# Second attention: the reciprocal row sums go through memory instead of through TensorE

## The chip, the cores and the metric

The program runs on one core of a Trainium2 chip. The metric is the device time of one execution in microseconds; the median of three executions stands for the kernel. Five engines run their own instruction streams and meet through semaphores: TensorE (PE), VectorE (DVE), ScalarE (ACT), GpSimd (POOL) and SyncE (SP), which here only issues DMAs. "L133" in a row of the profile is line 133 of the kernel. The lines named most often are those of one-line helpers (L133 matmul, L136 transpose, L139 activation, L142 tensor_tensor, L157 tensor_copy, L163 reciprocal, L193 dma_start), so a row says which kind of instruction it is, and its place in time says which one.

## The reference

Two transformer blocks follow each other on a 1024 x 1024 input. The change lies in the attention of the second block: 16 heads of 64 values, a window of 384 keys around each block of 128 queries, 256 context keys, and one sink term per head in the softmax.

```python
def block(i):
    ...
    s_lat = jnp.einsum('bqhgd,bshd->bhgqs', qb, kb).astype(jnp.float32) * scale
    s_ctx = jnp.einsum('bqhgd,bshd->bhgqs', qb, k_ctx).astype(jnp.float32) * scale
    ...
    logits = jnp.concatenate([s_lat, s_ctx, sink_column(sink, s_lat.shape[:-1])], axis=-1)
    p = jax.nn.softmax(logits, axis=-1)
    ...
    return (jnp.einsum('bhgqs,bshd->bqhgd', p_lat, vb)
            + jnp.einsum('bhgqs,bshd->bqhgd', p_ctx, v_ctx))
```

The kernel leaves the division by the softmax's row sums to the end: it multiplies the values with exp(score - max) and scales the result by the reciprocal of each row sum.

## The kernel before

All order is written out by hand: each engine has a function for each stage, and a table of named events gives the semaphores. The second attention is the stage `mix_*`. It takes 64 steps `s`, each for one query block and two heads; eight steps make one query block `i`, and four steps make a group `g = s // 4` (16 groups, eight heads each). Steps run in pairs.

- **PE** (`mix_pe`): for each pair of steps, `qk2` makes the scores of the next pair into PSUM banks 0 to 4; `turn2` transposes 128 x 128 pieces of exp(score), four per call, into banks 5 and 7 in turn (`turn_bank`); `turn_fifth` does the fifth piece where a block has five key tiles (blocks 1 to 6). Between them `fill_part` puts matmuls of another product (the projection of the convolution branch, 128 x 512 by three per part) that accumulates in bank 6. Where `s % 4 == 0`, `values2` multiplies the turned pieces of the group before with the values, into bank 7. The results stand with heads and value dimensions on the partitions and the 128 queries along the row.
- **Row sums.** DVE's `row_sums2(g)` leaves the eight reciprocals of a group in `rinv`, with queries on partitions. The result of `values2` has queries along its rows, so the reciprocals must be turned. Before the change POOL copies them out into `rspread`, 128 x 512, each value 64 times (`o2_spread`), and PE's `sums2(g - 1)` turns this with four transposes, at the end of the first pair of steps of group g. DVE's `o2_normed(g - 1)` multiplies `on` (the result, taken from PSUM by ACT's `o2_take`) with the turned reciprocals in PSUM, at the start of the second pair of group g.
- **DVE** (`mix_dve`) runs in order: `o2_normed`, `sink_arg`, then `max2` (mask and row maximum of the next scores, out of banks 0 to 4) interleaved with the copies of turned pieces (`p2_evacuate`), then `row_sums2` and `pc_take` at the end of the second pair. PE's next `qk2` waits for the last `max2` of the pair before, since it takes its banks.
- **SP** (`mix_sp`) issues the loads of a gate tile (`gs_load`, 256 KB, waits for `pc_take` of two groups before) and of the next weights (`w_load`, 512 KB) in one queue. **POOL** (`mix_pool`) issues `pc_store`, 256 KB per group.

After this stage come the output projection (`proj_*`), the router and the 16 experts.

Of the kernel before, what the change touches and what calls it, by code (L numbers as in the profile page):

```python
# [7 lines left out]
F32 = mybir.dt.float32  # L8
F32R = mybir.dt.float32r
U32 = mybir.dt.uint32  # L10
ALU = mybir.AluOpType
# [38 lines left out]
    
# [4 lines left out]
    "x_row_sums": "x1_half x2_half", "rope_step": "rope_swap rope_cos rope_sin",  # L55
}
# [169 lines left out]
def program(  # L226
# [7 lines left out]
    with ctx:  # L234
# [3 lines left out]
        def new_sem(name):  # L238
# [3 lines left out]
            nc.dram_tensor(f"{n}_scratch", [1024, 1024], F32, kind="Internal").ap()  # L242
            for n in ("x1", "x2", "xh", "xa", "y", "sa", "sc"))
        pc_dram = nc.dram_tensor("pc_scratch", [1024, 1024], F32, kind="Internal").ap()
        q_dram = nc.dram_tensor("q_scratch", [1280, 1024], F32, kind="Internal").ap()
        c_dram = nc.dram_tensor("c_scratch", [8, 1024], F32, kind="Internal").ap()
        h_dram = nc.dram_tensor("h_scratch", [2816, 1024], F32, kind="Internal").ap()
# [23 lines left out]
        def sm(*dims):  # L271
            n = int(np.prod(dims))
            v = small[:, taken[0]:taken[0] + n]
            taken[0] += n
            assert taken[0] <= 584, taken
            return shaped(v, dims)
# [4 lines left out]
        def rr(kb, *dims):  # L281
            return shaped(piece(AR0 + kb, int(np.prod(dims)), F32R), dims)
# [66 lines left out]
        W_PC = len(WT)  # L349
# [15 lines left out]
        def w_raw(n):  # L365
            _, nk, cols_, _ = WT[n]
            return piece(8 * (n % 2), 2048, F32)[:, 0:nk * cols_].rearrange("p (k n) -> p k n", n=cols_)
# [8 lines left out]
        def w_load(sp, n):  # L376
            parts, nk, cols_, _ = WT[n]
            if n >= 2:
                sp.wait_ge("w_low", n - 2)
            for place, src in parts:  # L380
                sp.dma_start(place(w_raw(n)), src).then_inc(*sp.landed(f"w_raw{n % 2}", n))
# [68 lines left out]
        def ps(sem, *key):  # L450
            return PS[:, bank_of.get((sem, *key), 0), :]
# [315 lines left out]
        rinv = sm(16)  # L767
# [856 lines left out]
        hs = [tuple(rr(32 + 4 * j + a, 512) for a in (0, 2)) for j in range(4)]  # L1624
# [779 lines left out]
        LAST = NST - 1  # L2404
# [560 lines left out]
        amask, amask0, rspread = ar(48, 640), ar(50.5, 512), ar(52.5, 4, 128)  # L2965
# [26 lines left out]
        def yh_of(h, k):  # L2992
            return yh[8 * h + k]
# [16 lines left out]
        def y_low(e, h, k):  # L3010
            e.wait_ge("y_high", h, k)
            e.tensor_tensor(yl_of[h][:, k, :], yl_raw[h][:, k, :], yh_of(h, k).bitcast(F32), ALU.subtract).then_inc(
                *e.did(y_low_of(h), h, k))
# [26 lines left out]
        def gs_load(sp, n):  # L3040
            if n >= 16:
                return
            if n >= 2:
                sp.wait_ge("pc_out", n - 2)
            else:
                sp.wait_ge("st_acc", LAST, "P2")
                for x in range(4):
                    sp.wait_ge(f"g_st{x}", 7)
            sp.dma_start(gs[n % 2], sc_dram[tile128(n // 2), half512(n % 2)]).then_inc(*sp.landed(f"gl{n % 2}", "c", n))

        def mix_sp(sp):
            gs_load(sp, 0)
            gs_load(sp, 1)
            for j in range(8):
                gs_load(sp, 2 * j + 2)
                if j < 7:
                    w_load(sp, W_PC + j + 2)
                gs_load(sp, 2 * j + 3)

        QK_PIECES = ((0, 1, 384, 640), (1, 0, 256, 640), (0, 0, 0, 256), (1, 1, 256, 640), (0, 0, 256, 512), (0, 0, 512, 640),  # L3060
                     (1, 0, 0, 256), (0, 1, 0, 256), (1, 1, 0, 128), (0, 1, 256, 384), (1, 1, 128, 256))
# [60 lines left out]
        def sums2(pe, g):  # L3122

            b = turn_bank(pe)
            pe.take(b, "o2_out", g)
            bank_of["o2_sums", g] = b
            pe.wait_ge("o2_spread", g)
            for j in range(4):
                t = pe.transpose(PS[:, b, tile128(j)], rspread[:, j, :], ident)
            t.then_inc(*pe.did("o2_sums", g))  # L3130
# [15 lines left out]
        def mix_pe(pe):  # L3146
            pe.wait_ge("k_in")
            pe.wait_ge(*v2_out(4))
            pe.wait_ge(*v2_out(5))
            pe.wait_ge("kc_out_a")  # L3150
            pe.wait_ge("kc_out_v")
            qk2(pe, 0)
            for s in range(2):
                for k1 in range(2):
                    fill_part(pe, s, k1)
            for s in range(0, NS2, 2):
                if s + 2 < NS2:
                    qk2(pe, s + 2)
                if s and s % 4 == 0:
                    values2(pe, s // 4 - 1)  # L3160
                if s % 4 == 0:
                    pe.turn = 0
                for s_ in (s, s + 1):
                    for c in range(2):
                        turn2(pe, s_, c)
                        if s:
                            fill_part(pe, s_, c)
                if len(chunks2(s)) == 3:
                    turn_fifth(pe, s)
                pe.named("p2_turned", s)  # L3170
                pe.named("p2_turned", s + 1)
                if s and s % 4 == 0:
                    sums2(pe, s // 4 - 1)
            values2(pe, 15)
            pe.turn = 0
            sums2(pe, 15)
            pe.turn = 0
# [93 lines left out]
        def o2_normed(dve, g):  # L3271

            dve.wait_ge("o2_taken", g)
            dve.wait_ge("o2_sums", g)
            dve.tensor_tensor(q2_of(g // 2)[:, 4 * (g % 2):4 * (g % 2) + 4, :], on[g % 2].rearrange("p (k n) -> p k n", n=128),
                              ps("o2_sums", g).rearrange("p (k n) -> p k n", n=128), ALU.mult).then_inc(*dve.did("o2_out", g))

        def pc_take(dve, n):
            dve.wait_ge("pc_acc", n)
# [53 lines left out]
        def mix_pool(pool):  # L3333
            for s in range(NS2):
                for h, k in y_parts(s):
                    if h:
                        y_low(pool, h, k)
                if s % 4 == 3:
                    g = s // 4
                    hs = slice(8 * (g % 2), 8 * (g % 2) + 8)  # L3340
                    pool.wait_ge("o2_rinv", g)
                    if g:
                        pool.wait_ge("o2_sums", g - 1)
                    pool.tensor_copy(rspread.rearrange("p j (a d) -> p j a d", d=64),
                                     rinv[:, hs].rearrange("p (a j) -> p j a", j=4).unsqueeze(3).to_broadcast(
                                         [128, 4, 2, 64])).then_inc(*pool.did("o2_spread", g))
                    pc_store(pool, g)

        def pc_store(pool, n):
            pool.wait_ge("pc_out", n)  # L3350
            pool.dma_start(pc_dram[tile128(n // 2), half512(n % 2)], pcb[n % 2]).then_inc(*pool.landed(f"pc_st{n % 2}", n))
# [975 lines left out]
        rows, ssr, rsr = xg, sm(3), sm(1)  # L4327
# [239 lines left out]
```

## Time and profile before

| | |
|---|---|
| median of 3 runs | 2761.48 us (2761.33 to 2762.14) |
| the profiled execution | 2762.24 us, span 2760.5 us |
| PE busy over the span | 2712.5 us, 98% |
| DVE busy | 1988.2 us, 72% |
| ACT busy | 1304.8 us, 47% |
| POOL busy | 547.1 us, 20% |
| granted TensorE clock | 0.996 of full speed on the mean |
| the chain that ended last | PE 86%, DVE 6%, DMA 2%, ACT 2%, issue 2%, POOL 2% |

The execution's own time is 1.7 us above its span: what lies around the first and last instruction. The busy share of PE is an average over all stages; how much of it is on the path in the second attention, from about 1664 to 1968 us, is read from the rows further down.

### The profile page before, as it was taken

Reading aid. Unit: us, or ns where it says so; the run is one execution under the profiler, and the core shown is the slowest. Engines: PE = TensorE matmul, PEld = TensorE weight load, DVE = VectorE, ACT = ScalarE, POOL = GpSimd, SP = SyncE. Lnnn points to the kernel's source line nnn. Section 1 sums busy time; section 2 is a strip of 40 time slices with the busy share of each in tenths; the row PEclk is TensorE's granted clock in tenths of the full one; section 3 lists DMA queues with packets and bytes.
Section 4 is the critical chain, followed back from the end, with each engine's and each line's share of the span. In section 5 each row is a group of like instructions: output and inputs, shape, how many; then the busy total and the mean of one; then the engine's idle time right before and its main releaser. Section 6 shows DMA issues by size and latency. Waiting matters only on the chain.

```text
span 2760.5 us, 35397 instructions
## 1 busy us (share of the span) xinstructions
PE 2712.5 (98%) x13762; PEld 2182.8 (79%) x13762; DVE 1988.2 (72%) x2820; ACT 1304.8 (47%) x2040; POOL 547.1 (20%) x512
## 2 busy tenths in 40 slices
PE   8999999999999999999999999999999899999998
PEld 7777778777778888988888887777788678888886
DVE  5344455888776588978867656666666889999997
ACT  5444533433333454443222236555423477777775
POOL 0011011645545111520011112000100410000000
PEclk9999999999999999999999999999999999999999
DMA  5111113344662898324312244011574699999998
GB/s 172 35 47 31 46 57 135 107 137 143 186 183 70 313 313 236 118 88 111 107 62 77 80 149 139 31 47 39 172 264 152 233 402 396 397 396 396 396 396 299
DMA packets 270634, 494.12 MB, mean 179 GB/s; under 512 B 30140, under 2 KB 141908, under 8 KB 269956
## 3 DMA queue, kind: packets, MB, share of 16 engines
q1 hardware_dynamic: 240864, 396.40, 41.2%
q0 software_dynamic: 29456, 95.43, 10.6%
q8 instruction: 109, 1.79, 0.3%
q14 instruction: 57, 0.47, 0.1%
q10 hardware_dynamic: 148, 0.04, 0.0%
HBM read 424.60 MB, written 67.21 MB: 178 GB/s over the span
## 4 chain that ended last, share of the span: by engine, by line
PE 86%; DVE 6%; DMA 2%; ACT 2%; issue 2%; POOL 2%; POOLq 0%; SPq 0%; DVEq 0%; ACTq 0%
PE PS L133 80%; PE PS L136 6%; DVE m L142 4%; ACT m L139 2%; POOL m L142 2%; DVE m L148 1%; DMA m<-h_scratch 1%; DMA m<-xh_scratch,small 0%; DMA m<-in_w_mod_dram 0%; DMA xa_scratch<-m,small 0%; ACT L139 0%; DVE m L151 0%; DVE m L145 0%; DMA m<-in_w_exp_up_dram 0%; DMA m<-in_x_dram 0%
## 5 line engine op out<-in xcount | busy, mean ns | idle before, releaser
L133 PE MATMUL PS<-m,m 128*128 128x512 f32 (+6 forms) x11722 | 2507.8, 387 | 10.2 <-DVE m L142 5.0
L133 PEld LDWEIGHTS PS<-m,m 128*128 128x128 f32 (+2 forms) x11722 | 1961.8, 183 | 465.1 <-issue 76.5
L139 ACT ACTIVATE m<-m 128x512 fp32r<-128x512 f32 (+4 forms) x887 | 797.2, 919 | 880.5 <-DVE m L142 379.3
L142 DVE TENSOR_TENSOR m<-m,m 128x512 fp32r<-128x512 f32 (+5 forms) x912 | 986.3, 1112 | 211.5 <-ACT m L139 189.9
L139 ACT ACTIVATE m<-PS 128x512 f32<-128x512 f32 (+4 forms) x495 | 278.2, 588 | 388.1 <-PE PS L133 188.1
L142 DVE TENSOR_TENSOR m<-PS,m 128x512 f32<-128x512 f32 (+1 forms) x454 | 299.8, 684 | 177.6 <-PE PS L133 119.8
L142 POOL TENSOR_TENSOR m<-m,m 128x512 f32<-128x512 f32 (+4 forms) x178 | 278.5, 1569 | 603.3 <-DVE m L142 273.3
L136 PE MATMUL PS<-ident,m 128*128 128x128 f32 x1722 | 245.1, 277 | 22.8 <-DVE m L145 8.6
L136 PEld LDWEIGHTS PS<-ident,m 128*128 128x128 f32 x1722 | 199.7, 141 | 76.6 <-issue 28.5
L139 ACT ACTIVATE m<-m,small 128x640 f32<-128x640 f32 (+5 forms) x203 | 157.6, 780 | 117.3 <-DVE small L151 116.5
L157 DVE COPY m<-PS 128x512 f32<-128x512 f32 (+2 forms) x148 | 95.4, 648 | 142.0 <-PE PS L136 116.3
L148 DVE SCALAR_TENSOR_TENSOR m<-m,small,m 128x512 f32<-128x512 f32 (+1 forms) x154 | 168.2, 1116 | 4.3 <-DMA x_scratch<-m 1.7
L151 DVE CUSTOM_DVE_ANT_0 m<-PS,m,small 128x640 f32<-128x640 f32 (+1 forms) x128 | 102.3, 845 | 26.7 <-PE PS L133 26.7
L148 DVE SCALAR_TENSOR_TENSOR m<-m,vecT,m 128x512 fp32r<-128x512 f32 (+3 forms) x96 | 63.4, 715 | 53.4 <-ACT m L139 52.8
L142 POOL TENSOR_TENSOR m<-m 128x512 f32<-128x512 f32 x62 | 83.9, 1361 | 30.0 <-DMA m<-in_w_gate_up_dram 17.8
L151 DVE CUSTOM_DVE_ANT_0 m<-PS,m 128x1024 f32<-128x1024 f32 (+7 forms) x64 | 45.9, 754 | 58.8 <-PE PS L133 58.8
L199 POOL DMA_INDIRECT m<-xh_scratch,small x17 | 22.2, 1308 | 253.3 <-PE PS L136 246.8
L142 DVE TENSOR_TENSOR m<-m,PS 128x512 f32<-128x512 f32 x75 | 50.8, 684 | 28.7 <-PE PS L133 15.9
L199 POOL DMA_INDIRECT xa_scratch<-m,small x15 | 27.4, 1827 | 208.6 <-DVE m L148 208.6
L139 ACT ACTIVATE m<-m,vecT 128x512 fp32r<-128x512 f32 (+2 forms) x80 | 41.3, 599 | 44.3 <-PE PS L133 44.2
L157 POOL COPY m<-small 128x512 f32<-128x512 f32 x16 | 9.9, 616 | 254.7 <-DVE small L163 254.7
L142 DVE TENSOR_TENSOR m<-m 128x512 f32<-128x512 f32 (+1 forms) x57 | 40.7, 714 | 0.1
(107 smaller groups left out, 547.3 us busy)
## 6 DMA issues: line engine op xcount, KB each, us to landing
m<-in_w_exp_gate_dram SPq DMA_DIRECT2D x64, 1024.0 KB, 15.2
m<-in_w_exp_up_dram SPq DMA_DIRECT2D x64, 1024.0 KB, 14.7
m<-in_w_exp_down_dram SPq DMA_DIRECT2D x64, 1024.0 KB, 15.0
m<-in_w_mod_dram SPq DMA_DIRECT2D x48, 512.0 KB, 3.8
m<-in_w_gate_up_dram SPq DMA_DIRECT2D x44, 512.0 KB, 6.6
m<-in_w_in_dram SPq DMA_DIRECT2D x21, 1024.0 KB, 5.2
m<-in_w_in_dram SPq DMA_DIRECT2D x25, 512.0 KB, 5.2
x_scratch<-m POOLq DMA_DIRECT2D x24, 512.0 KB, 3.8
```

The lines of the kernel that those rows point to most:

```text
L133: return Unsent() if self.e is None else self.e.matmul(o, l, r, start=first, stop=last, **k)
L136: return Unsent() if self.e is None else self.e.transpose(o, i, ident)
L139: return Unsent() if self.e is None else self.e.activation(o, i, fn, **k)
L142: return Unsent() if self.e is None else self.e.tensor_tensor(o, a, b, op)
L148: return Unsent() if self.e is None else self.e.scalar_tensor_tensor(out=o, in0=a, scalar=s, in1=b, op0=op0, op1=op1, **k)
L151: return Unsent() if self.e is None else self.e.tensor_tensor_reduce(**k)
L157: return Unsent() if self.e is None else self.e.tensor_copy(o, i)
L199: return Unsent() if self.e is None else self.e.indirect_dma_start(*a, **k)
```

## The change

For the groups 0 to 14, the spreading by POOL and the four transposes by PE go. SP gets three DMAs per group in their place: `spread_store` writes the 128 x 8 values of `rinv` as eight rows of 128 into a scratch tensor in memory, and `spread_load` reads rows 0 to 3 back onto partitions 0 to 63 and rows 4 to 7 onto partitions 64 to 127 of `rspread`, 2 KB per partition. `o2_normed` multiplies with `rspread` in SBUF instead of a PSUM bank. Group 15 keeps the old way. `pe.turn`, which picks bank 5 or 7, is set back at every pair of steps and no longer at every second.

```diff
+        rs_dram = nc.dram_tensor("rs_scratch", [8, 128], F32, kind="Internal").ap()
...
+        def spread_store(sp, g):
+            if g > 14:
+                return
+            sp.wait_ge("o2_rinv", g)
+            if g:
+                sp.wait_ge("rs_in", g - 1, 1)
+            with nc.allow_non_contiguous_dma(reason="eight values of each partition go to eight rows"):
+                sp.dma_start(rs_dram.rearrange("r q -> q r"), rinv[:, 8 * (g % 2):8 * (g % 2) + 8]).then_inc(
+                    *sp.landed("rs_st", g))
+
+        def spread_load(sp, g):
+            if g > 14:
+                return
+            sp.wait_ge("rs_st", g)
+            if g:
+                sp.wait_ge("o2_out", g - 1)
+            else:
+                sp.wait_ge("st_acc", LAST, "P2")
+            for a in range(2):
+                sp.dma_start(rspread[64 * a:64 * a + 64].rearrange("p j n -> p (j n)"),
+                             rs_dram[4 * a:4 * a + 4].rearrange("r q -> (r q)").partition_broadcast(64)).then_inc(
+                    *sp.landed("rs_in", g, a))
+
         def mix_sp(sp):
             gs_load(sp, 0)
             gs_load(sp, 1)
             for j in range(8):
-                gs_load(sp, 2 * j + 2)
-                if j < 7:
-                    w_load(sp, W_PC + j + 2)
-                gs_load(sp, 2 * j + 3)
+                for g in (2 * j, 2 * j + 1):
+                    spread_store(sp, g)
+                    gs_load(sp, g + 2)
+                    spread_load(sp, g)
+                    if g % 2 == 0 and j < 7:
+                        w_load(sp, W_PC + j + 2)
...
-                if s % 4 == 0:
-                    pe.turn = 0
+                pe.turn = 0
...
-                if s and s % 4 == 0:
-                    sums2(pe, s // 4 - 1)
...
             dve.wait_ge("o2_taken", g)
-            dve.wait_ge("o2_sums", g)
+            if g < 15:
+                dve.wait_ge("rs_in", g, 1)
+                inverses = rspread
+            else:
+                dve.wait_ge("o2_sums", g)
+                inverses = ps("o2_sums", g).rearrange("p (k n) -> p k n", n=128)
             dve.tensor_tensor(q2_of(g // 2)[:, 4 * (g % 2):4 * (g % 2) + 4, :], on[g % 2].rearrange("p (k n) -> p k n", n=128),
-                              ps("o2_sums", g).rearrange("p (k n) -> p k n", n=128), ALU.mult).then_inc(*dve.did("o2_out", g))
+                              inverses, ALU.mult).then_inc(*dve.did("o2_out", g))
...
+                if s == 63:
+                    pool.wait_ge("o2_rinv", 15)
+                    pool.wait_ge("o2_out", 14)
+                    pool.tensor_copy(rspread.rearrange("p j (a d) -> p j a d", d=64),
...
                 if s % 4 == 3:
-                    g = s // 4
-                    hs = slice(8 * (g % 2), 8 * (g % 2) + 8)
-                    pool.wait_ge("o2_rinv", g)
-                    if g:
-                        pool.wait_ge("o2_sums", g - 1)
-                    pool.tensor_copy(rspread.rearrange("p j (a d) -> p j a d", d=64),
...
-                    pc_store(pool, g)
+                    pc_store(pool, s // 4)
```

On PE, in a block with five key tiles, this is what stands between the first and the second pair of a group, with the semaphores waited for. `m_178` and `m_180` hold exp(score) of the fifth pieces, `m_176` is `rspread`, and `m_147` by `m_124` is the first matmul of `qk2`.

```order
@@ -6781,6 +6779,4 @@
 L136 MATMUL PS<-ident,m_178 128x128
 L136 MATMUL PS<-ident,m_180 128x128
-L136 MATMUL PS<-ident,m_176 128x128 [waits s_o2_spread,s_p_out_v]
-L136 MATMUL PS<-ident,m_176 128x128 x3
 L133 MATMUL PS<-m_147,m_124 128x256 [waits s_s_max]
```

Four transposes go and nothing takes their place; `qk2` follows `turn_fifth` directly, with the wait that it had.

On SP, this is the queue from the second gate tile to the first loads of group 1. `small` is where `rinv` lies, `m_208` and `m_209` are the gate tiles, and `s_y_dma` and `s_x_dma` count the new store and the new loads.

```order
 L193 DMA m_209<-sc_scratch 128x512
+L193 DMA rs_scratch<-small 128x8x1 [waits s_o2_rinv]
 L193 DMA m_208<-sc_scratch 128x512 [waits s_pc_out]
+L193 DMA m_176<-rs_scratch 64x512 [waits s_y_dma]
+L193 DMA m_176<-rs_scratch 64x512
 L193 DMA m_148<-in_w_proj_conv_dram 128x8x128 [waits s_w_low]
+L193 DMA rs_scratch<-small 128x8x1 [waits s_x_dma,s_o2_rinv]
 L193 DMA m_209<-sc_scratch 128x512 [waits s_pc_out]
+L193 DMA m_176<-rs_scratch 64x512 [waits s_o_out,s_y_dma]
+L193 DMA m_176<-rs_scratch 64x512
```

The store goes ahead of the gate tile's load; the two loads go behind it and ahead of the weights' load, and they wait for the store to land.

On DVE, the rows of `o2_normed` (the multiplication into `m_124`) between the copies of the first pair and `sink_arg` and `max2` of the second:

```order
 L157 COPY m_186<-PS 128x4x128 [waits s_o_acc,s_p_turned]
 L157 COPY m_186<-PS 128x4x128 [waits s_p_turned]
-L142 TENSOR_TENSOR m_124<-m_49,PS 128x512 [waits s_o2_sums,s_o2_taken]
+L142 TENSOR_TENSOR m_124<-m_49,m_176 128x512 [waits s_x_dma,s_o2_taken]
 L142 TENSOR_TENSOR small<-small 128x8 [waits s_s_max]
```

Its place is the same; it now waits for the loads' semaphore instead of PE's.

## Rows read from the trace of the kernel before

**Rows 1.** Windows: the 280 us of the stage's steady part
```profile
core 0: us, PE busy (x) PEld busy (x) DVE busy (x) ACT busy (x) POOL busy (x), PEclk, DMA share, GB/s
1680.00:1960.00 280.00, 280.00 (x1866) 204.39 (x1863) 171.75 (x378) 152.08 (x341) 22.88 (x35) 1.00 0.14 45
```
**Rows 2.** Chain of waits, one group: start us, us, what, instructions
```profile
1823.79 0.87 PE PS L136 x8
1824.66 2.37 PE PS L133 x18
...
1831.69 0.44 PE PS L136 x4
```
**Rows 3.** Groups by shape in 1680 to 1960: count, busy, mean ns
```profile
L142 DVE TENSOR_TENSOR m<-m,PS 128x512 f32<-128x512 f32 x15 | 10.3, 689 | 12.7 <-PE PS L136 12.7
```
**Rows 4.** Timeline of DVE, groups 7 and 8: start, duration, [idle before]
```profile
1813.16 0.20 DVE L163 RECIPROCAL small<-small 128x8 f32<-128x8 f32 x1
1813.28 0.68 DVE L142 TENSOR_TENSOR m<-PS,m 128x512 f32<-128x512 f32 x1
...
1823.14 0.69 DVE L157 COPY m<-PS 128x512 f32<-128x512 f32 x1 [1.56 <-PE PS L136]
1824.77 0.69 DVE L142 TENSOR_TENSOR m<-m,PS 128x512 f32<-128x512 f32 x1 [0.94 <-PE PS L136]
1825.38 0.16 DVE L142 TENSOR_TENSOR small<-small 128x8 f32<-128x8 f32 x1
1827.09 0.88 DVE L151 CUSTOM_DVE_ANT_0 m<-PS,m,small 128x640 f32<-128x640 f32 x1 [1.55 <-PE PS L133]
...
1830.19 0.88 DVE L151 CUSTOM_DVE_ANT_0 m<-PS,m,small 128x640 f32<-128x640 f32 x1
...
1832.96 0.20 DVE L163 RECIPROCAL small<-small 128x8 f32<-128x8 f32 x1
```
**Rows 5.** Timeline of POOL and of SP's queue, after the reciprocal
```profile
1813.43 0.62 POOL L157 COPY m<-small 128x512 f32<-128x512 f32 x1 [18.43 <-DVE small L163]
...
1813.99 20.12 SPq L193 DMA_DIRECT2D m<-sc_scratch  x2
```
**Rows 6.** Issue (ns) and landing of w_gate_up's loads, then of sc_scratch's
```profile
L193 SPq DMA_DIRECT2D m<-in_w_gate_up_dram x44: 367/548/882, 417.2 to 861.6; - x44
...
DMA to landing us min/median/max: 4.0/6.6/10.2
...
L193 SPq DMA_DIRECT2D m<-sc_scratch x16: 320/320/2758, 1671.2 to 1932.4; - x16
...
DMA to landing us min/median/max: 2.3/3.0/7.1
```
**Rows 7.** DMA queues over the whole span: packets, MB, share of 16 engines
```profile
q1 hardware_dynamic: 240864, 396.40, 41.2%
q0 software_dynamic: 29456, 95.43, 10.6%
```
**Rows 8.** Groups by shape on DVE in 1960 to 2050
```profile
L142 DVE TENSOR_TENSOR m<-m,m 128x512 f32<-128x512 f32 x14 | 9.7, 693 | 0.5
```
**Rows 9.** Timeline of DVE, groups 14 and 15
```profile
1948.92 0.20 DVE L163 RECIPROCAL small<-small 128x8 f32<-128x8 f32 x1
...
1960.99 0.69 DVE L157 COPY m<-PS 128x512 f32<-128x512 f32 x1 [0.73 <-PE PS L136]
```
**Rows 10.** Timelines of SP's queue and of ACT: two weights' loads, their first users
```profile
1794.55 0.43 SPq L193 DMA_DIRECT2D m<-in_w_proj_conv_dram  x1
...
1832.03 1.04 ACT L139 ACTIVATE m<-m 128x1024 fp32r<-128x1024 f32 x1
...
1932.74 21.07 SPq L193 DMA_DIRECT2D m<-in_w_proj_attn_dram  x8
...
1968.29 7.29 ACT L139 ACTIVATE m<-m 128x512 fp32r<-128x512 f32 x13
```
**Rows 11.** Issues of the experts' gate weights: first and last start
```profile
L193 SPq DMA_DIRECT2D m<-in_w_exp_gate_dram x64: 367/368/1057, 2113.9 to 2682.3; - x64
```

More of the change, by code:

```diff
@@ L3337, in mix_pool @@
                         y_low(pool, h, k)
-                if s % 4 == 3:
-                    g = s // 4
-                    hs = slice(8 * (g % 2), 8 * (g % 2) + 8)
-                    pool.wait_ge("o2_rinv", g)
-                    if g:
-                        pool.wait_ge("o2_sums", g - 1)
-                    pool.tensor_copy(rspread.rearrange("p j (a d) -> p j a d", d=64),
-                                     rinv[:, hs].rearrange("p (a j) -> p j a", j=4).unsqueeze(3).to_broadcast(
-                                         [128, 4, 2, 64])).then_inc(*pool.did("o2_spread", g))
-                    pc_store(pool, g)
+                if s == 63:
+                    pool.wait_ge("o2_rinv", 15)
+                    pool.wait_ge("o2_out", 14)
+                    pool.tensor_copy(rspread.rearrange("p j (a d) -> p j a d", d=64),
+                                     rinv[:, 8:16].rearrange("p (a j) -> p j a", j=4).unsqueeze(3).to_broadcast(
+                                         [128, 4, 2, 64])).then_inc(*pool.did("o2_spread", 15))
+                if s % 4 == 3:
+                    pc_store(pool, s // 4)
         def pc_store(pool, n):
```

2 rows, old and new, of the table SHARED are left out of this document.

## The prediction

> **What bounds the kernel now.** I read first how full each engine is in this stage, then the chain that ended last, then the engines' own timelines around one group.
>
> In the stage's steady part PE is busy for 280.00 of 280 us at full granted clock, DVE for 171.75, ACT for 152.08, and the DMA engines for 0.14 of their time [rows 1]. So PE is the only engine without idle time here, and the chain of waits agrees: inside a group it stays on PE from end to end. At the place of the change it shows eight transposes in one piece, the four of `turn_fifth` and the four of `sums2`, for 0.87 us, and `qk2` right behind; at the end of the next pair, where there is no `sums2`, four transposes take 0.44 us [rows 2]. What is taken off PE there is therefore on the path, as long as nothing that PE waits for comes later than now.
>
> What PE waits for next runs through DVE. The reciprocal of group 7 starts at 1813.16 and ends at 1813.36; `o2_normed(7)` starts at 1824.77, after 0.94 us of waiting for PE's transposes; `sink_arg` follows, and then DVE waits 1.55 us for the scores before `max2` starts at 1827.09 [rows 4]. That wait is the cushion behind `o2_normed`. The other cushion is ahead of it: from 1813.36 until DVE has finished the copy of 1823.14 (1823.83) there are 10.5 us in which nobody asks for the turned reciprocals.
>
> **What is removed.** On PE, four transposes for each of 15 groups. The chain gives 0.87 - 0.44 = 0.43 us for one group, and 0.44 for four transposes alone [rows 2]. 15 x 0.435 = 6.5 us, all on the path. On POOL, 15 spreads of 0.62 us [rows 5]; POOL is idle for 18.43 us ahead of each, so this is worth nothing.
>
> **What is exchanged on DVE.** `o2_normed` reads `rspread` from SBUF instead of a PSUM bank. With PSUM it takes 689 ns [rows 3]; the same shape with both operands in SBUF takes 693 ns in the next stage [rows 8]. 15 x 0.004 = 0.06 us on an engine that waits: nothing. The bank changes of `pe.turn` are nothing too: in blocks 1 to 6 the pairs before used 5, 7, 5, 7, 5 and then 7 for the sums, and the next pair began with 5 again, so dropping the 7 leaves the rest as it was. In blocks 0 and 7 the second pair now begins with 5 instead of 7, a bank whose last copy is three fills and a `qk2` old.
>
> **What is added: a longer way from `rinv` to `rspread`.** It has these steps.
>
> 1. SP wakes and issues the store. POOL's spread started 0.07 us after the reciprocal's end, SP's gate load 0.03 us after `pc_take`'s end (1813.28 + 0.68 = 1813.96, issue 1813.99) [rows 4, 5]. I take 0.1 us.
> 2. The store lands, L us after its issue. No DMA here writes pieces of 4 bytes. It has 128 x 8 = 1024 pieces, 64 for each of the 16 DMA engines. A load of `w_gate_up` also has 1024 pieces (512 KB in runs of 128 values) and lands in 4.0 us at least, 6.6 in the middle; the shortest landing of a 256 KB tile, with 128 pieces, is 2.3 us [rows 6]. Lower end: 2.3 us, since the data are next to nothing. Upper end: the 2.3 us and 64 pieces at the price of a mean packet. A packet of the hardware queue costs 0.412 x 16 x 2760.5 / 240864 = 0.0755 us, one of the software queue 0.106 x 16 x 2760.5 / 29456 = 0.159 us [rows 7], which makes 4.8 or 10.2 us of pieces, and L = 7.1 or 12.5 us. I take L = 4.0 us, the row with the same number of pieces with least beside it, as the DMA engines are nearly idle here [rows 1].
> 3. The gate tile's load stands between store and loads; its condition (`pc_take`) is met 0.6 us after the reciprocal, long before the store has landed. Nothing.
> 4. SP wakes (0.03), issues the first load (0.32), then the second, which lands after the 3.0 us that a gate tile takes in the middle [rows 6]: 3.35 us.
>
> The way is 0.1 + L + 3.35 = L + 3.45 us, so 7.5 us with L = 4.0. `rspread` is then ready at 1813.36 + 7.5 = 1820.8. DVE comes to `o2_normed` at 1823.83 less the 0.44 us by which PE is now ahead, 1823.4. It does not wait; even the 0.94 us that it waited for PE goes.
>
> **How much of L is free.** DVE does not wait at all up to L = 10.0 - 3.45 = 6.6 us. If it waits, what stands behind it is `sink_arg` and `max2`. The latest harmless start of `o2_normed` is 1827.09 - 0.44 - 0.61 - 0.16 = 1825.88, 12.5 us after the reciprocal. Behind it DVE runs without a gap until the last `max2` ends at 1830.19 + 0.88 = 1831.07, and PE's `qk2`, which needs it, starts at 1831.69 + 0.44 = 1832.13 [rows 2, 4]: 1.05 us more. So PE loses nothing up to 13.55 us, or L = 10.1. The groups of blocks 0 and 7 are shorter. For group 14 the reciprocal ends at 1949.12 and DVE's next copy after `o2_normed` and `sink_arg` (0.77 together) starts at 1960.99 [rows 9]: 11.1 us, 10.7 with PE ahead, so L = 7.2 before that copy is late, and about 1 us more before PE is. I expect the same of groups 0 and 13.
>
> **What is moved in SP's queue.** The weights' load now stands behind the loads of even groups, some L + 1 us later than before. The load issued at 1794.55 is first used by ACT at 1832.03, 37 us later [rows 10]. After group 14 the projection's second load can no longer be issued at 1932.74, it comes behind the loads of group 14: 1949.12 + 0.1 + 4.0 + 0.7, about 1954. Its first user on ACT stands in the run that starts at 1968.29 [rows 10]; 14 us cover a landing of 6.6. With L = 12.5 it would still be 5 us before. Nothing.
>
> **What comes after.** The first expert weights are asked for at 2113.9 [rows 11], after this stage, and everything later starts from its end, so the rest shifts as a whole.
>
> **Sum.** 2761.48 - 6.5 = 2755.0 us as a median. The profiled execution took 2762.24 us with a span of 2760.5, 0.8 above the median; one like it would show 2755.7 and a span of 2754.0.
>
> **A rule against the change.** What the rows say of the store is in step 2: no packet here costs more than 0.159 us on the mean of its queue [rows 7], and with that the loss is small or none. The Trainium skill says (VectorE: DVE Perf Modes, "The three transpose paths") that a plain DMA that transposes by its strides is 19 times slower than the transposing path, where the innermost destination stride is large, which is what the store does. With that page's 1.3 us for the fast path the store would take about 25 us, an estimate from the page alone; no run here shows it.
>
> **Rivals.**
>
> - *The store's narrow writes are slow, and DVE waits (ends slower).* Place: `o2_normed`, with `sink_arg` and `max2` behind it, and PE's `qk2` behind those. For it: no such DMA is in the trace, and DVE serves nobody while it waits. Against it: 64 pieces per DMA engine would have to cost over (10.1 - 2.3) / 64 = 0.12 us each. At 0.159 us, L = 12.5 is 2.4 us over in 12 groups and about 4.3 in the three short ones: 41.7 - 6.5 = 35 us slower, 2797. It breaks even at 6.5 / 15 = 0.43 us over per group, L = 10.5. Chance 0.10. *In an extreme form* a piece costs 0.35 us, twice the dearest mean: L = 2.3 + 22.7 = 25, 15 us over in 15 groups, 223 - 6.5: 2978 us. Chance 0.02. That is the size that the Trainium skill's rule of 19 times gives.
> - *The freed time is lost elsewhere (no change).* PE comes 0.44 us sooner to its next waits, and one of them fills it. For it: all engines hang on each other here. Against it: the only wait directly behind is that of `qk2` on a `max2` from the pair before, and DVE sat idle for 0.94 and 1.55 us in between [rows 4]. 2761.5 us, chance 0.05.
> - *Half of it.* The short groups are late by some tenths, or the later stages give back a part, as the DMA traffic of the experts falls otherwise: 2757 to 2760. Chance 0.10.
> - *More than counted*, from the shorter wait at `o2_normed` or POOL's quiet: below 2754. Chance 0.03.
>
> **How the numbers follow.** The forecast, 2755.0 with 2754 to 2756.5 as its own range, has 0.70. Two executions of this kernel agree within 0.03%, and I count 0.2%, 5.5 us, as the least that can be told from no change; the border is 2755.96, only 1 us above the forecast. So of the 0.70 I give 0.62 to faster by over 0.2% and 0.08 to within it; with 0.03 of the larger gain faster has 0.65. Within 0.2%: 0.08 + 0.10 + 0.05 = 0.23. Slower: 0.12. The range from 2753.5 to 2760.0 leaves out the slow store, no change and a little of the rest, 0.2 in all.
>
> **What would show it.** Right: between the pairs of a group PE has four transposes and `qk2` right behind, PE stays busy for all of the steady part, and the reciprocals of two groups in blocks 1 to 6 lie 19.36 us apart instead of 19.80 (1813.16 to 1832.96) [rows 4]. `o2_normed` has no wait for a DMA; the store lands in 3 to 6 us. Wrong in its size: the store lands in over 6.6 us and `o2_normed` shows a wait for the load, though PE doesn't. Wrong in sign: the store lands in over 10 us, PE waits for DVE at `qk2`, and the groups lie over 19.80 us apart.

## The result, and the profile after

The changed kernel takes 2816.47 us (median of 4 executions, 2815.3 to 2820.19) against 2761.68 before: 1.0198 times as long, interval 1.0186 to 1.0211, so 55 us slower where 6.5 us faster was forecast. Its profiled execution took 2820.19 us with a span of 2818.2.

The stage is where it went. The windows of the changed kernel, to compare with [rows 1]:

```profile
core 0: us, PE busy (x) PEld busy (x) DVE busy (x) ACT busy (x) POOL busy (x), PEclk, DMA share, GB/s
1680.00:1700.00 20.00, 16.07 (x93) 11.88 (x91) 8.59 (x21) 9.60 (x22) 5.92 (x7) 0.88 0.28 66
1700.00:1960.00 260.00, 231.08 (x1425) 166.09 (x1424) 132.16 (x293) 120.97 (x259) 6.28 (x12) 0.94 0.25 45
1960.00:2025.00 65.00, 56.30 (x328) 37.33 (x326) 30.12 (x71) 28.01 (x64) 2.23 (x4) 0.95 0.37 61
```

PE, full before, is idle for 41.5 of 345 us, its granted clock is below 1, and the DMA engines are busier (0.25 against 0.14) while they move as little. The experts' first load, which answers to [rows 11], starts at 2171.7 instead of 2113.9: all of the 57.7 us between the two spans is lost by then.

```profile
L193 SPq DMA_DIRECT2D m<-in_w_exp_gate_dram x64: 367/368/1453, 2171.7 to 2740.5; - x64
```

The list of waits from 1680 to 2020 says for whom (waiter, who was waited for, us in total, times, longest):

```profile
DVE m L142 <- DMA m<-rs_scratch: 86.8, 15, 6.9
...
PE PS L136 <- DVE m L157: 39.0, 14, 3.9
```

DVE waits 15 times for the loads of the reciprocals, 5.8 us each, and behind it PE waits 14 times for a copy on DVE, 2.8 us each. The chain of waits shows what the way from `rinv` is made of (start, us, what), for one group:

```profile
1815.89 10.33 DMA rs_scratch<-small
1826.22 0.02 issue
1826.24 0.45 SPq L193
1826.69 0.04 issue
1826.73 5.72 DMA m<-rs_scratch
...
1832.54 0.10 DVE m L142
```

The store takes 10.33 us, over all groups 9.9 to 12.3; then the second load takes 5.72. From the first load's issue to `o2_normed` it is 6.3 us here and in the middle of the groups, and 3.8 to 6.8 over all of them. From the reciprocal's end at 1815.86 to `o2_normed` at 1832.54 it is 16.7 us, 3.1 more than the 13.55 that were worked out as free. DVE's timeline has the wait where [rows 4] had 0.94 us for PE:

```profile
1825.64 0.69 DVE L157 COPY m<-PS 128x512 f32<-128x512 f32 x1 [1.56 <-PE PS L136]
1832.54 0.69 DVE L142 TENSOR_TENSOR m<-m,m 128x512 f32<-128x512 f32 x1 [6.21 <-DMA m<-rs_scratch]
1833.15 0.16 DVE L142 TENSOR_TENSOR small<-small 128x8 f32<-128x8 f32 x1
```

PE's timeline has the consequence, 2.95 us of waiting at a `turn2` that takes bank 7, with DVE's copy out of it still behind two `max2`:

```profile
1830.21 0.60 PE L136 MATMUL PS<-ident,m 128*128 128x128 f32 x4
...
1835.58 1.12 PE L136 MATMUL PS<-ident,m 128*128 128x128 f32 x4 [2.95 <-DVE m L157]
1836.35 1.63 PE L133 MATMUL PS<-m,m 128*128 128x512 f32 x3
1837.77 1.01 PE L136 MATMUL PS<-ident,m 128*128 128x128 f32 x4
1838.71 6.88 PE L133 MATMUL PS<-m,m 64*128 64x256 f32 x42
```

The four transposes after the wait take 1.12 us, those before it 0.60. A window over these shows the clock (columns as above):

```profile
1832.60:1835.50 2.90, 0.03 (x1) 0.00 (x0) 2.90 (x8) 1.56 (x4) 0.00 (x0) 0.95 0.09 25
1835.50:1838.70 3.20, 3.12 (x11) 2.46 (x11) 2.23 (x6) 2.59 (x7) 0.00 (x0) 0.51 0.00 0
```

PE stood still for 2.9 us and then worked at 0.51, the lower of its two levels (1.2 GHz), for 3.2 us; in the windows before (1829.0 to 1832.4) and after (1838.7 to 1845.0) it has 1.00, the full 2.4 GHz. From 1835.58 to 1838.71 it needs 3.13 us for what takes 1.66 in the kernel before (from the transposes at 1810.60 to `qk2` at 1812.26). So this group costs 2.95 for the wait and 1.5 for the clock. Not every group pays for the clock. Windows laid behind each of the 15 waits of the stage (40.0 us together) show the lower level behind 11 of them; behind the waits of 0.92, 1.99 and 0.99 us it stayed at the full one, and also behind one of the longest, 3.69 us (PE's timeline, and a window with the columns as above):

```profile
1741.55 0.65 PE L136 MATMUL PS<-ident,m 128*128 128x128 f32 x4 [3.69 <-DVE m L157]
```

```profile
1741.55:1748.55 7.00, 7.00 (x47) 4.55 (x49) 6.41 (x16) 4.26 (x11) 0.54 (x1) 1.00 0.07 1
```

Over the stage the three windows at the top give the bill: 41.5 us of idle PE, and 20 x 0.12 + 260 x 0.06 + 65 x 0.05 = 21 us for the clock, less the 6.5 us of the transposes: 56 of the 57.7 us. The stores of 12 groups lie between 1721.36 and 1981.61, 23.7 us apart, against 19.37 when nothing waits (below): 4.3 us more per group.

### The profile page after: what moved, and what is told of

Same layout as the page of the kernel before. It is cut to its first block, busy times and chain, and to the rows that moved or that the text cites. A ratio compares the mean times of both kernels' runs of the same rounds, so it can differ in the third digit from the quotient of the medians.

```text
span 2818.2 us, 35306 instructions
## 1 busy us (share of the span) xinstructions
PE 2728.4 (97%) x13702; PEld 2190.0 (78%) x13702; DVE 1985.9 (70%) x2820; ACT 1309.7 (46%) x2040; POOL 537.6 (19%) x497
## 3 DMA queue, kind: packets, MB, share of 16 engines
q0 software_dynamic: 29456, 95.43, 10.5%
## 4 chain that ended last, share of the span: by engine, by line
PE 75%; DMA 10%; DVE 9%; issue 3%; ACT 2%; POOL 1%; SPq 0%; POOLq 0%; DVEq 0%; ACTq 0%
PE PS L133 71%; DMA rs_scratch<-small 6%; DVE m L142 4%; PE PS L136 4%; DMA m<-rs_scratch 3%; ACT m L139 1%; DVE m L151 1%; DVE m L148 1%; POOL m L142 1%; DVE m L157 1%; DMA m<-in_w_down_dram 0%; DVE m L187 0%; DVE m L190 0%; DMA m<-xh_scratch,small 0%; DMA m<-in_w_mod_dram 0%
## 5 line engine op out<-in xcount | busy, mean ns | idle before, releaser
L142 DVE TENSOR_TENSOR m<-m,m 128x512 fp32r<-128x512 f32 (+4 forms) x927 | 996.5, 1105 | 296.6 <-ACT m L139 190.6
L136 PE MATMUL PS<-ident,m 128*128 128x128 f32 (+1 forms) x1662 | 246.1, 283 | 64.6 <-DVE m L157 41.5
L136 PEld LDWEIGHTS PS<-ident,m 128*128 128x128 f32 (+1 forms) x1662 | 197.0, 144 | 124.0 <-DVE m L157 49.1
L151 DVE CUSTOM_DVE_ANT_0 m<-PS,m,small 128x640 f32<-128x640 f32 (+1 forms) x128 | 102.3, 846 | 11.4 <-PE PS L133 11.2
L193 POOL DMA_DIRECT2D pc_scratch<-m x16 | 8.7, 544 | 307.4 <-DVE m L142 307.2
L142 DVE TENSOR_TENSOR m<-m,PS 128x512 f32<-128x512 f32 x60 | 40.5, 684 | 15.9 <-PE PS L133 15.9
```

The source lines that it names most:

```text
L136: return Unsent() if self.e is None else self.e.transpose(o, i, ident)
L142: return Unsent() if self.e is None else self.e.tensor_tensor(o, a, b, op)
L151: return Unsent() if self.e is None else self.e.tensor_tensor_reduce(**k)
L193: return Unsent() if self.e is None else self.e.dma_start(o, i)
```

## The experiments

Where a kernel leaves something out, its expectation says it. The kernel before ran beside each on the same chip (medians 2762.03 to 2762.31), and the ratios are against it. Of each store the table at the end gives the time from its issue to the first load's issue, both rows of SP's queue, for groups 1 to 14; it is called the store's time here.

**The store in pieces of 32 bytes** (e1_wide)

```diff
-                sp.dma_start(rs_dram.rearrange("r q -> q r"), rinv[:, 8 * (g % 2):8 * (g % 2) + 8]).then_inc(
...
+            sp.dma_start(rs_dram.rearrange("r (a b) -> (r a) b", b=8), rinv[:, 8 * (g % 2):8 * (g % 2) + 8]).then_inc(
...
```

> The changed kernel with one edit: the store writes each partition's eight reciprocals as one piece of 32 bytes (128 pieces), so the rows read back hold them in another order and the output is not the reference's. Same bytes, same waits, same loads. Theory A (the 1024 pieces of 4 bytes are what makes the store take 10 to 12 us): the store lands in 2 to 3 us, the loads after it in about 3.3, o2_normed does not wait, and the time is that of the first forecast, 2755 (2754 to 2757). Theory B (two DMAs behind each other through memory are too slow in any form, or share the queue with too much): the store stays above 6 us or the loads above 5, and the time stays above 2780. Gate tile loads, 13 us in the changed kernel, fall back to 3 us by A.

2755.81 us, ratio 0.9976 (0.9967 to 0.9986). The loads follow the store's issue by 1.4 us (less than the 2 to 3 expected), the gate tile's loads land in 3.0 us in the middle again, no wait for the reciprocals' loads is left, and PE is busy for 279.82 of the 280 us. The same two hops with the same bytes are hidden: theory A holds, B is out.

**No DMAs at all** (e2_no_dma)

```diff
-                    spread_store(sp, g)
                     gs_load(sp, g + 2)
-                    spread_load(sp, g)
...
-                dve.wait_ge("rs_in", g, 1)
                 inverses = rspread
```

> The changed kernel without the store and the loads: o2_normed of groups 0 to 14 multiplies with a tile that is set to 1.0 once, so the division by the row sums is left out for these groups. It measures the gain term alone. Theory A (PE's 60 transposes were all on the path at 0.435 us per four, and nothing else takes their place): 6.5 us faster than before, 2755.2 (2754.5 to 2756), groups of blocks 1 to 6 19.36 us apart. Theory B (the freed PE time is lost to another wait): 2760 or more, with a PE wait in the trace at qk2 or turn2.

2757.6 us, ratio 0.9983 (0.9974 to 0.9992), 4.5 us faster with an interval of 2.2 to 7.2 that holds the 6.5; the median lies above the range of theory A (2754.5 to 2756). The timeline measures the term more sharply. Two reciprocals in a row:

```profile
1810.27 0.20 DVE L163 RECIPROCAL small<-small 128x8 f32<-128x8 f32 x1
...
1829.64 0.20 DVE L163 RECIPROCAL small<-small 128x8 f32<-128x8 f32 x1
```

19.37 us instead of 19.80 [rows 4], 0.43 per group as read from [rows 2], and the span of the profiled execution is 2754.3 against 2760.5. The gain term was right.

**The kernel before, with the store added** (e3_before_store)

```diff
+                    spread_store(sp, g)
                     gs_load(sp, g + 2)
...
+            if g >= 2:
+                dve.wait_ge("rs_st", g - 2)
```

DVE's added wait keeps `rinv` from being overwritten before it is stored.

> The kernel before, with its four transposes kept, and the store of 1024 narrow pieces added for groups 0 to 14; nobody reads what it writes. Theory A1 (the loss comes only through DVE's wait for the loads): 2761.7, within 2 us of before, although the store lands in 10 us or more. Theory A2 (the narrow store also costs by holding up the DMA engines for the other transfers): the gate tile's load and pc_store land in 10 us or more as in the changed kernel, but since they are wanted two groups later, the time still stays within 3 us of before; over 2770 would say that the hold-up itself costs.

2761.78 us, ratio 0.9997 (0.9988 to 1.0007). The gate tile's loads land in 12.8 us in the middle between 1700 and 1960 us (3.0 before) and `pc_store` in 13.1 (3.5 before), but the gate tiles are wanted two groups later, and what `pc_store` writes only in the next stage. The narrow stores hold up the other transfers, and that alone costs nothing here: A1 holds, and of A2 the hold-up is there, without a cost.

**DVE turns, then four stores** (e4_dve_turn)

```diff
+            dve.reciprocal(rp[:, g % 2, 0:8], rinv[:, hs]).then_inc(*dve.did("dve_order~"))
+            dve.wait_ge("dve_order~")
+            dve.blocks_turned(rt[:, g % 2, :], rp[:, g % 2, :]).then_inc(*dve.did("o2_rinv", g))
...
+            for b in range(4):
+                sp.dma_start(rs_dram[:, 32 * b:32 * b + 32], rt[32 * b:32 * b + 8, g % 2, :]).then_inc(
+                    *sp.landed("rs_st", g, b))
```

> The changed kernel with the turning done by DVE ahead of the store: the eight reciprocals stand in 32 columns, DVE turns the four 32 x 32 blocks in one instruction, and four stores of 8 pieces of 128 bytes each write the rows; loads and everything else as in the changed kernel, and the whole computation is kept. Theory A: DVE pays about 0.2 us per group, the last of the four stores lands about 1.1 + 2.5 us after the first issue, rspread is ready some 8 us after the reciprocal, inside the 10 us that are free, and the time is 2755 (2754 to 2757.5), faster than both kernels. Theory B (any round trip through memory is too slow here): above 2770, with o2_normed waiting for the loads.

2755.8 us, ratio 0.9977 (0.9968 to 0.9986): faster than both kernels, with the whole computation. SP's queue and DVE:

```profile
1810.14 1.30 SPq L196 DMA_DIRECT2D rs_scratch<-m  x4
1811.48 0.34 SPq L196 DMA_DIRECT2D m<-sc_scratch  x1
1812.35 1.09 SPq L196 DMA_DIRECT2D m<-rs_scratch  x2
```

```profile
1809.90 0.21 DVE L181 STREAM_TRANSPOSE m<-m 128x32 f32<-128x32 f32 x1
...
1819.65 0.69 DVE L157 COPY m<-PS 128x512 f32<-128x512 f32 x1 [1.56 <-PE PS L136]
1820.26 0.68 DVE L142 TENSOR_TENSOR m<-m,m 128x512 f32<-128x512 f32 x1
```

The turn costs 0.21 us, the loads are issued 2.2 us after the first of the four stores, and `o2_normed` follows the copy without a wait.

**The pieces 512 bytes apart** (e5_apart)

```diff
+                sp.dma_start(rs_apart[:, :, 0], src).then_inc(*sp.landed("rs_st", g))
```

> The changed kernel with the store's 1024 pieces of 4 bytes written 512 bytes apart, each to a stretch of its own in a larger scratch tensor; the loads wait for it as before but read rows that only group 0 wrote, so the output is not the reference's. Theory C (the writes are slow because neighbouring pieces of one row, from different DMA engines, meet in the same stretch of memory): the store lands in 2.5 to 4 us and the time is about 2756. Theory D (each 4-byte write to memory costs about (10.3 - 2.3) / 64 = 0.125 us on its DMA engine wherever it goes): the store still takes about 10 us and the time stays near 2816.

2756.67 us, ratio 0.9978 (0.9968 to 0.9988). There are still 1024 pieces of 4 bytes, and one partition's eight stand 512 bytes apart in memory, as in the changed kernel, but the next partition's piece is 4096 bytes away and not 4; the loads follow the store's issue by 3.4 us. Theory D, the price per piece on its DMA engine, is out; it matters where the pieces go.

**Four of eight values** (e6_half)

```diff
+                sp.dma_start(rs_dram[0:n].rearrange("r q -> q r"), rinv[:, 8 * (g % 2):8 * (g % 2) + n]).then_inc(
...
```

> The changed kernel, but from group 1 on the store writes four of the eight values of each partition (512 pieces of 4 bytes), so the other four rows stay those of group 0 and the output is not the reference's. Theory D (price per piece): the store lands in 2.3 + 32 x 0.125 = 6.3 us, rspread is ready some 11 us after the reciprocal, DVE waits about 1 us and PE not at all, and the time is 2755 to 2758. Theory E (a fixed price for a store of such a form, whatever its number of pieces): 9 us or more, and the time stays above 2800.

2782.12 us, ratio 1.0066 (1.005 to 1.0081). Half the pieces take nearly as long, 10.0 us in the middle: D is out here too. Theory E has the store right and the time wrong (over 2800 expected). The time is shorter than the changed kernel's mostly through the loads: from the first load's issue to `o2_normed` it takes 4.5 us in the middle, against 6.3, and PE waits for 20 us in all where it waited for 40. That the loads find less ahead of them fits the gate tile's loads (9.8 us in the middle, 13.3 in the changed kernel) but was not tested by itself.

**The gate tile behind the loads** (e7_gate_behind)

```diff
+                    spread_load(sp, g)
                     gs_load(sp, g + 2)
-                    spread_load(sp, g)
```

> The changed kernel with the load of the gate tile moved behind the two loads of the reciprocals in SP's queue. Theory F (the loads take 5 to 6 us instead of 3.3 because the gate tile's packets, held up by the narrow store, still stand ahead of them): they land in 3.3 to 4 us, the way from the reciprocal to rspread falls from some 16.8 to 14.4 us, 0.9 over the 13.5 that are free, and the time falls to 2765 to 2785. Theory G (the DMA engines are still busy with the store's aftermath and with pc_store, so the order in SP's queue does not matter): above 2800.

2787.42 us, ratio 1.009 (1.0075 to 1.0106), 2 us above the range of F and far from G. The store is as slow as before (10.7 us), but the loads land in 3.1 us in the middle (4.5 in the changed kernel), so most of what the 5.7 us had over that was the gate tile's load ahead of them in the queue, held up by the store. This is half of the loss, 29 of 55 us: PE waits 18 us less in all, and the lower clock follows 3 waits and no longer 11.

**`o2_normed` asked for later** (e8_asked_later)

```diff
-                    if g:
-                        o2_normed(dve, g - 1)
                     sink_arg(dve, g)
...
                     pc_take(dve, g)
+                    if g:
+                        o2_normed(dve, g - 1)
```

> The changed kernel, the whole computation kept, with DVE's multiplication o2_normed moved from the start of the second pair of a group to the end of the pair, behind row_sums2 and pc_take, about 9 us later. Store and loads are those of the changed kernel. Theory A (only DVE's wait, placed ahead of max2, makes the kernel slow): rspread is ready some 17 us after the reciprocal and asked for after about 19, nothing waits, and the time is 2755.5 (2754.5 to 2757). Theory H (the narrow store slows the stage in other ways too, the late gate tiles for one): above 2765.

2757.61 us, ratio 0.9981 (0.9972 to 0.999), the whole computation, with the slow store kept (9.5 us in the middle); it is 0.6 us above the range of theory A and far from H. Theory H is out: the loss comes only through DVE's wait ahead of `max2`.

**What makes the store slow.** Six more stores, each with the loads and waits of the changed kernel. Half the queries (e12_half_queries):

```diff
+                sp.dma_start(rs_dram.rearrange("r q -> q r")[0:n], rinv[0:n, 8 * (g % 2):8 * (g % 2) + 8]).then_inc(
...
```

> The changed kernel, but from group 1 on the store writes all eight rows for 64 of the 128 queries: again 512 pieces of 4 bytes as in the run with four of eight values, where the store did not get faster (8.2 to 11.1 us). The other half of each row stays that of group 0, so the output is not the reference's. Theory S (the pieces of one row of 512 bytes are written one after another, about (10.3 - 2.3) / 128 = 0.06 us each, and the rows beside each other, so the number of pieces per row sets the time): 64 pieces per row, the store lands in about 2.3 + 4 = 6.3 us and the time is 2755 to 2759. Theory E (a fixed price for this form of store): about 10 us and a time near that of the other half, 2782.

2789.71 us, ratio 1.0095 (1.0078 to 1.0112). Theory S is out: with 64 instead of 128 pieces in a row the store still takes 9.8 us. Theory E, about 10 us and a time near 2782, comes closest.

Then the pieces 16, 64 and 8 bytes apart in each row (e11_apart16, e9_apart64, e13_apart8), into a scratch tensor `rs_apart` of [8, 128, 4], [8, 128, 16] and [8, 128, 2]:

```diff
+                sp.dma_start(rs_apart[:, :, 0].rearrange("r q -> q r"), src).then_inc(*sp.landed("rs_st", g))
```

> The changed kernel with the store's 1024 pieces written 16 bytes apart in each row, so that 32 pieces share 512 bytes and 4 share 64 bytes, from different DMA engines; the loads read rows that only group 0 wrote, so the output is not the reference's. Theory S: 32 x 0.06 = 2 us of queueing, the store lands in 4 to 5 us, and the time is 2755 to 2758. Theory N (it is enough that several DMA engines write near each other, whatever the number): 8 us or more and over 2780.

2757.26 us, ratio 0.9978 (0.9969 to 0.9988); 3.5 us. N is out.

> The same with the pieces 64 bytes apart in each row: 8 share 512 bytes, none share 64 bytes. Theory S: 8 x 0.06 = 0.5 us, the store lands in 2.8 to 3.5 us, time 2755 to 2758, as with pieces 512 bytes apart. Theory N: 8 us or more and over 2780.

2756.25 us, ratio 0.9977 (0.9967 to 0.9986); 3.0 us.

> As the runs with pieces 16 and 64 bytes apart in each row, now 8 bytes apart, so that 8 pieces from different partitions share 64 bytes (16 in the changed kernel, 4 at 16 bytes apart); the loads read rows that only group 0 wrote, so the output is not the reference's. Theory P (the number of pieces that share a stretch of some 64 bytes sets the time: 1 gave 3.0 us from the store's issue to the loads', 4 gave 3.4, 16 gave 10.4): 5 to 6 us, as the run with eight pieces of one partition in 64 bytes had with 5.2, and the time is 2755 to 2758, since up to 10 us is free. Theory X (what costs is that neighbouring pieces come from different DMA engines): clearly over the 5.2 us of that run, 7 us or more.

2755.0 us, ratio 0.9976 (0.9967 to 0.9986); 4.5 us, a little under the 5 to 6 of theory P. Eight pieces of one partition take 5.2 (e10_own_line, below, which was run first), so that neighbours come from different partitions is not what costs: X is out. Which DMA engine carries which piece, of which the expectations speak, no trace here shows.

Last, each partition's pieces by themselves, into [128, 64, 2] (e10_own_line), and packed from a constant tile into [128, 8] (e14_own_dense):

```diff
+                sp.dma_start(rs_apart[:, 0:8, 0], src).then_inc(*sp.landed("rs_st", g))
```

```diff
+                sp.dma_start(rs_apart, sinkr[:, 0:16:2]).then_inc(*sp.landed("rs_st", g))
```

> The same with each partition's eight pieces 8 bytes apart within 64 bytes, and the partitions 512 bytes apart: 8 pieces share 512 bytes as in the run with 64 bytes, but now they share one stretch of 64 bytes too, and all eight come from one partition and so one DMA engine. If pieces queue by the stretch of 512 bytes, the store lands as fast as there (2.8 to 3.5 us). If they queue by the stretch of 64 bytes, at (10.3 - 2.3) / 16 = 0.5 us for each of the 16 pieces that share one in the changed kernel, it takes 2.3 + 8 x 0.5 = 6.3 us. The time is 2755 to 2758 either way.

2756.93 us, ratio 0.998 (0.997 to 0.999); 5.2 us, 2.2 more than with the pieces 64 bytes apart, though as many share 512 bytes: the stretch of 512 bytes is out, and the 6.3 of the other reading is 1.1 too high.

> The store writes 1024 pieces of 4 bytes from every second value of a constant tile, each partition's eight pieces next to each other (32 bytes), so memory is as densely written as in the changed kernel, 16 pieces to 64 bytes, but neighbours come from one partition or the next one, not from 128 partitions. The loads wait for it and read rows that only group 0 wrote, so the output is not the reference's. Theory P (density alone): 9 to 11 us from the store's issue to the loads', and a time over 2780. Theory X (different DMA engines, or partitions far apart in the engines' order, have to meet in one stretch): 5 us or less and a time of 2755 to 2758.

2757.24 us, ratio 0.9983 (0.9973 to 0.9992); 7.3 us. Neither theory: as dense as the changed kernel and clearly slower than every thinner store, but 3 us short of 10.5. It writes the same places as e1_wide, where each partition's 32 bytes are one piece and not eight: 1.4 us there, 7.3 here. So narrow pieces are slow without any turning too. Two rows of SP's queue each, first of the store with pieces 64 bytes apart, then of this one:

```profile
1770.07 0.36 SPq L193 DMA_DIRECT2D rs_apart<-small  x1
...
1773.02 1.09 SPq L193 DMA_DIRECT2D m<-rs_scratch  x2
```

```profile
1811.22 0.55 SPq L193 DMA_DIRECT2D rs_apart<-small  x1
...
1818.26 1.09 SPq L193 DMA_DIRECT2D m<-rs_scratch  x2
```

| store | pieces | how many share 64 bytes | us from store to loads: least, middle, most |
|---|---|---|---|
| changed kernel | 1024 | 16, different partitions | 9.9, 10.5, 12.1 |
| four of eight values | 512 | 16, different partitions | 8.2, 10.0, 11.1 |
| half the queries | 512 | 16, different partitions | 9.0, 9.8, 11.4 |
| packed, from one partition after another, out of another tile | 1024 | 16, two partitions | 6.6, 7.3, 9.7 |
| 8 bytes apart, partitions 512 apart | 1024 | 8, one partition | 4.2, 5.2, 5.7 |
| 8 bytes apart | 1024 | 8, different partitions | 4.2, 4.5, 5.0 |
| 16 bytes apart | 1024 | 4, different partitions | 2.6, 3.5, 4.3 |
| 64 bytes apart | 1024 | 1 | 2.6, 3.0, 4.0 |
| 512 bytes apart | 1024 | 1 | 2.9, 3.4, 3.6 |
| four stores of 128 byte pieces | 32 | none | 2.2, 2.2, 2.4 |
| 32 byte pieces | 128 | 2, two partitions | 1.4, 1.4, 2.4 |

## Why the prediction was wrong

- **Bound and gain: right.** PE was the only full engine, and 15 groups of four transposes at 0.435 us were on the path: without the DMAs' wait the groups lie 19.37 us apart, 19.36 was forecast.
- **Step 2, "I take L = 4.0 us, the row with the same number of pieces": the step that failed.** The store took 10.5. The count of pieces was the wrong likeness: 1024 pieces of 4 bytes with 64 bytes to each land in 3.0 us, below the 4.0 taken, and 512 pieces packed together take 10. The load of `w_gate_up` differs from this store in that it reads memory, and in pieces of 512 bytes; what makes the store slow is that 4-byte pieces lie next to each other. The trace of before had no row for it. The upper bound, 7.1 to 12.5 from mean packets, did hold the 10.5, by a reasoning that the half stores refute: that is luck. The lower end, 2.3 us, was misread too: the row of [rows 6] mixes the gate tile's loads with the stores that filled the same scratch tensor through POOL's queue, and the 2.3 is of a store; the loads alone take 2.8 at least, 3.0 in the middle.
- **Steps 3 and 4, nothing for the gate tile and 3.35 us for the loads: failed with it.** It came to 6.3 in the middle. That the gate tile's condition is met was right, but its load takes 13.3 us behind the slow store, and the reciprocals' loads stand behind it; with the gate tile behind them (e7_gate_behind) it is 4.2. This matters as much as step 2: by the prediction's own sum a store of 10.5 us alone only breaks even, at 2761.5.
- **"PE loses nothing up to 13.55 us": right in size, wrong in place.** At 16.7 us PE waits 2.95, and 16.7 - 13.55 = 3.1. The wait is at a `turn2` whose bank DVE has yet to copy out, not at `qk2`. Where nothing waits (e4_dve_turn) the copy is done 0.9 us before that `turn2` starts, and the last `max2` 1.0 us before `qk2`, so the two cushions are alike.
- **The rival of the slow store: right in kind, with a term missing.** Its 2797 had L = 12.5 and an excess of 2.4 us in most groups. The excess was about 3.1, with a shorter store and longer loads, and PE's time at the lower clock, 21 us in the stage, was not in it. Its signs of a wrong sign did come: the store over 10 us, the groups over 19.80 us apart.
- **The rule of the Trainium skill** (VectorE: DVE Perf Modes, "The three transpose paths") pointed the right way here: it says that a plain DMA that turns by its strides is slow where the innermost destination stride is large. The 25 us, an estimate from its time for a 128 x 128 bf16 tile, do not occur; the runs here show 10.5. The innermost stride in memory is 512 bytes in the changed kernel and in e5_apart, and the store takes 10.5 and 3.4 us, so the stride alone is not what costs.
- **The other steps** (POOL's spread, SBUF instead of PSUM at `o2_normed`, the banks, the weights' loads moved in SP's queue) cost nothing that shows, as PE is busy for 279.82 of 280 us in e1_wide and e4_dve_turn.

Open stays why the densest store takes 10.5 us from 128 partitions and 7.3 from neighbouring ones; the second also reads another tile, with steps of 8 bytes, and no run separates the two. That several 4-byte writes to one short stretch of memory are done one after another fits the table, but no run shows the memory itself, and the stretch of 64 bytes is the unit in which I counted, not one that was measured.

## What to carry to other kernels

A DMA off the path has a deadline, not a price: work out from the timeline when its result is asked for and what its slowest form would take, and if no row shows that form, measure the store by itself first. Turn data before it is stored, so that the pieces are tens of bytes long (one 0.21 us turn on DVE did it), or ask for the result later. Look also at what stands behind a slow DMA in its queue: the gate tile's load made half of the loss. And an engine that waits longer than its cushion can pay twice: PE paid 41.5 us for standing still and 21 for the lower clock that followed 11 of its 15 waits.

## What the runs showed that I had not expected

- A store of 4 KB in packed 4-byte pieces holds up transfers of other queues: `pc_store` goes through POOL's queue, and its landing went from 3.5 us in the middle to 13.9 between 1700 and 1960 us, that of the gate tile's load from 3.0 to 13.4. In e3_before_store, where only the store is added, they are 13.1 and 12.8; in e1_wide, 3.4 and 3.0.
- A 4 KB store in 128 pieces of 32 bytes is followed by its reader 1.4 us after its issue; a load of a 256 KB gate tile took at least 2.8 in the kernel before.
- 2.95 us of waiting on PE were followed by 3.2 us at a granted clock of 0.51, and a wait of 1.89 us in e7_gate_behind by the lower clock too, while one of 3.69 us in the changed kernel was not. What decides it stays open here.
